# A mixture-of-experts block on one core: the 32-row activations turned by VectorE in 32x32 blocks, with weight rows dealt to partitions to match

## What is computed

```
logits = xf @ w_router + b_router            # 32 experts
top_val, top_idx = top_k(logits, 4); gates = softmax(top_val)
# for each token and each of its four experts e:
hu   = x @ w1[e] + b1[e]                      # 1024 -> 2048: gate 1024, lin 1024
gate = min(hu[:1024], 7); lin = clip(hu[1024:], -7, 7)
act  = gate * sigmoid(1.702 * gate) * (lin + 1)
out += gates[e] * (act @ w2[e] + b2[e])       # 1024 -> 1024
```

## Time and profile before

| what | value |
|---|---|
| median of 3 runs (lowest to highest) | 1412.05 us (1411.45 to 1412.62) |
| span of the profiled execution | 1411.9 us |
| TensorE busy | 1306.3 us (93%) |
| VectorE busy | 654.5 us (46%) |
| ScalarE / GpSimd busy | 292.9 / 296.0 us (21% each) |
| bytes moved by DMA | 459.19 MB |
| first `up` matmul | at 367.8 us of the span |

### The profile page before, as it was taken

One profiled execution on the slowest core, in us unless ns is written; L12 is line 12 of the kernel. 1 busy time (PEld: TensorE's weight loads), 2 busy tenths in 40 slices (PEclk: granted clock), 3 DMA queues, 4 the chain that ended last, 5 costly groups with the idle time before them and its releaser, 6 DMA issues.

```text
span 1411.9 us, 36717 instructions
## 1 busy us (share of the span) xinstructions
PE 1306.3 (93%) x13322; PEld 635.0 (45%) x13323; DVE 654.5 (46%) x2237; ACT 292.9 (21%) x582; POOL 296.0 (21%) x475
## 2 busy tenths in 40 slices
PE   7999999989579996999999999997999799999992
PEld 4756665555134442444444444442444344444441
DVE  2114334655545552555555555553555355555555
ACT  2012223424111110111111111111111111111113
POOL 5310000002122221222222222221222122222221
PEclk9999999999789998999999999999999999999997
DMA  9520003427498999999999997999999999999994
GB/s 322 145 50 1 1 0 139 164 82 283 192 415 358 415 417 421 415 419 416 418 416 416 417 414 303 380 411 417 420 417 419 418 417 416 416 418 415 418 416 171
DMA packets 59954, 459.19 MB, mean 325 GB/s; under 512 B 8693, under 2 KB 9077, under 8 KB 27157
## 3 DMA queue, kind: packets, MB, share of 16 engines
q1 hardware_dynamic: 51364, 436.12, 74.6%
q0 software_dynamic: 8176, 22.36, 6.0%
q10 hardware_dynamic: 384, 0.32, 0.1%
HBM read 440.26 MB, written 18.51 MB: 325 GB/s over the span
## 4 chain that ended last, share of the span: by engine, by line
PE 83%; DMA 10%; DVE 3%; issue 2%; ACT 1%; POOL 0%; SPq 0%; DVEq 0%; ACTq 0%; POOLq 0%
PE PS L1682 38%; PE PS L1709 19%; DMA sb_arena<-in_w 7%; PE PS L1347 4%; PE PS L1341 4%; PE PS L1719 2%; PE PS L1344 2%; PE PS L1345 2%; PE PS L1541 2%; PE PS L1663 1%; DMA xfd<-sb_arena 1%; PE PS L1725 1%; PE PS L1689 1%; PE PS L1392 1%; PE PS L1514 1%
## 5 line engine op out<-in xcount | busy, mean ns | idle before, releaser
L1682 PE MATMUL PS<-sb_arena,sb_work 128*32 128x512 f32 x5184 | 590.0, 606 | 39.3 <-DMA sb_arena<-in_w 29.6
L1682 PEld LDWEIGHTS PS<-sb_arena,sb_work 128*32 128x32 f32 x5184 | 187.3, 112 | 391.9 <-issue 329.6
L1709 PE MATMUL PS<-sb_arena,sb_work 128*32 128x256 f32 x5184 | 298.3, 382 | 4.5
L1236 DVE TENSOR_SCALAR sb_work<-PS 128x256 f32<-128x256 f32 x81 | 34.2, 422 | 397.2 <-PE PS L1689 397.2
L1709 PEld LDWEIGHTS PS<-sb_arena,sb_work 128*32 128x32 f32 x5184 | 167.0, 110 | 112.0 <-issue 20.9
L831 ACT ACTIVATE sb_work<-PS 128x256 f32<-128x256 f32 x81 | 31.0, 383 | 816.1 <-PE PS L1719 816.1
L1249 DVE TENSOR_SCALAR sb_work<-PS,sb_gates 32x256 f32<-32x256 f32 x324 | 155.0, 478 | 11.1 <-PE PS L1709 2.0
L584 POOL TENSOR_TENSOR sb_sm<-sb_sm 128x1 f32<-128x1 f32 x85 | 16.7, 197 | 552.2 <-DVE sb_gidx L1190 547.0
L1160 DVE TENSOR_SCALAR sb_slots<-sb_ca,sb_b,sb_rk 128x128 bf16<-128x128 f32 x340 | 95.3, 368 | 59.1 <-issue 59.1
L593 POOL DMA_INDIRECT accd<-sb_work,sb_sidc x81 | 110.9, 1369 | 12.5 <-issue 1.1
L829 ACT ACT_TABLE_LOAD x81 | 103.9, 1283 | 1.4
(11 more groups left out here) (264 smaller groups left out, 1169.6 us busy)
## 6 DMA issues: line engine op xcount, KB each, us to landing
sb_arena<-in_w SPq DMA_DIRECT2D x192, 2048.0 KB, 19.7
sb_arena<-in_w_in SPq DMA_DIRECT2D x6, 2048.0 KB, 21.0
sb_arena<-in_x SPq DMA_DIRECT2D x8, 512.0 KB, 7.9
sb_arena<-in_w_out SPq DMA_DIRECT2D x2, 2048.0 KB, 11.9
accd<-sb_arena SPq DMA_DIRECT2D x4, 512.0 KB, 8.9
xfd<-sb_arena SPq DMA_DIRECT2D x4, 512.0 KB, 5.8
sb_arena<-accd SPq DMA_DIRECT2D x4, 512.0 KB, 5.4
out<-sb_arena SPq DMA_DIRECT2D x4, 512.0 KB, 3.5
```

Of the source, the lines that this page charges most:

```text
L1682: last = mm(PS[group(c), b, :].rearrange("p (a n) -> p a n", a=2), xT[:, k % 2, group(k // 2)], w[:, k, :, c, :], start=k == 0, stop=False)
L1709: last = mm(PS[group(n), 4, 0:QD], actT[:, k % 2, group(k // 2)], w[:, k, n * QD:(n + 1) * QD], start=False, stop=k == KT - 1)
```

## The change

The four PE transposes of a block and the two copies of ScalarE go. In their place VectorE turns 128x256 elements with one instruction that transposes each 32x32 block by itself. Such a turn does not move anything between partition groups, so column 32-groups of the activation end up as rows of the contraction only if the columns were dealt to the partition groups in the right way; the layouts follow from that.

- x: the columns of a token's row are written to the table in another order (`quartered(stage)` <- `quarters(res)`), and `ffn_norm` is loaded from an input that the host has permuted in the same way (`ffn_row`). The row of the last token tile, one VectorE instruction of 1024 columns, becomes four of 256.
- hidden: `up` lets partition group c have columns a*512 + c*128 + n with a = 0..3 and n < 128 (before a*1024 + c*256 + n with a = 0, 1 and n < 256). The w2 rows follow: a partition now gets four neighbouring rows, 16 KB in one piece.
- waits: `turn_rows` is inside `hidden` of the block before, between the clip and the product; `turn_hidden` of block g+1 stands behind `outputs` of block g. What waited for `xT_done` (SyncE at L482, GpSimd's gathers) waits for `xT_ready`.

```
-            return I["w2"][e, 2 * c * QD:2 * (c + 1) * QD, :].rearrange("(c p j) n -> p c j n", c=2, j=2)
+            return I["w2"][e, 2 * c * QD:2 * (c + 1) * QD, :].rearrange("(p j) n -> p j n", j=4)
...
-            sp.wait_ge(xT_done, 2)
+            sp.wait_ge(xT_ready, 2)
...
-                act.activation(stage[t % 2], res[:, t, :], ACT.Copy, scale=rinv[:, t:t + 1]).then_inc(scaled, 1)
+                act.activation(quartered(stage[t % 2]), quarters(res[:, t, :]), ACT.Copy, scale=rinv[:, t:t + 1])\
+                    .then_inc(scaled, 1)
...
-                        act.wait_ge(actT_done, g + 1)
-                        act.activation(actT, PS[:, 6, 0:QD].rearrange("p (j n) -> p j n", j=2), ACT.Copy)\
-                            .then_inc(actT_ready, 1)
...
-                        xT_copy(g + 2, b)
...
+            for q in range(Q):
+                nc.vector.scalar_tensor_tensor(quartered(stage[1])[:, q], quarters(res[:, 3, :])[:, q], rinv[:, 3:4],
+                                               quartered(gain)[:, q], ALU.mult, ALU.mult).then_inc(xf_last, 1)
...
+            def turn_rows(b, r):
+                dve.wait_ge(xg_in[b], r * 16 + 16)
+                nc.vector.transpose(xT.rearrange("p (c j) s -> p c j s", j=2),
+                                    xg[b].rearrange("p (c q j) -> p c j q", c=Q, j=2)).then_inc(xT_ready, 1)
+
+            def turn_hidden(n, b):
+                dve.wait_ge(act_ready, n + 1)
+                nc.vector.transpose(actT.rearrange("p (c j) s -> p c j s", j=4),
+                                    gat[b].rearrange("p (c q j) -> p c j q", c=2, j=4)).then_inc(actT_ready, 1)
...
                 nc.vector.tensor_scalar(lin, lin, HID_LIMIT, -HID_LIMIT, ALU.min, ALU.max).then_inc(hid_step, 1)
+                turn_rows(1 - b, r)
                 dve.wait_ge(sig_ready, n + 1)
...
                         outputs(g, b)
+                        with dve.If(g + 1 < nb):
+                            turn_hidden(g + 1, 1 - b)
+                        dve.nop()
                         selector(g + 2, b)
...
-                        last = mm(PS[group(n), 4, 0:QD], actT[:, k % 2, group(k // 2)],
+                        last = mm(PS[group(n), 4, 0:QD], actT[:, k, :],
...
-                pe.wait_ge(act_ready, g + 1)
-                for j in range(2):
-                    last = nc.tensor.transpose(PS[:, 6, j * P:(j + 1) * P], pairs(gat[b], j), ident)
-                last.then_inc(actT_done, 1)
-                turn_x(g + 2, b, i + 1)
```

69 lines of the change are left out of this document (30 added, 39 removed).

## The result

The changed kernel takes 1405.11 us (median of 13 runs, 1400.21 to 1409.34). The ratio to the kernel before is 0.9936, with a 95% interval of 0.9921 to 0.9950: some 9 us faster (7 to 11), where the forecast was 16. The median lies inside the forecast's range of 1389 to 1406, at its upper end. The profiled execution has a span of 1403.6 us, 8.3 less than before. One of the 20 executions of the kernel before that stand beside the first four experiments took 2289 us, at a granted clock of 0.602, and the ratios leave it out.

A forecast was written before the change was run, and what follows sets the result against it. The prediction took the weight loads as the bound, with TensorE close beside; +1 (start) - 5 (w2) - 7 (free time filled) - 5 (tail) = -16 from 1411.9 us gave 1396 us, range 1389 to 1406.

The forecast's parts named there:

- The start: First weight loads wait for VectorE's turn of block 1: stream 5 us later, mostly absorbed at 424 to 432; net +1 us.
- The pieces: Loads of w2 in 16 KB pieces: 0.085 us saved on each of 63 loads in the full stretches, -5 us.
- The free time from 857 on: Free DMA time from 857 to 902, 9.7 us, mostly filled because TensorE releases buffers earlier: -7 us, ends -3 and -9.7.
- the lead: How much earlier TensorE lets the load of 864.19 be issued: 8 to 9 us, so at about 855.5.
- The tail: After the last weight load lands: last `down` ends 2.3 to 2.8 us behind it instead of 7.8; -5 us.
- TensorE, 0.58 for a block: Between `up` and `down`, without the four transposes: each block 0.58 us shorter, 11.20 in place of 11.78.
- VectorE, nothing: VectorE's two turns in each block, 0.42 us each (0.3 to 1.1), are covered and add no time.
- the cover: VectorE's slack in each block before TensorE waits: 3.4 us for two turns beyond 0.36 idle; each us beyond counts 81 times.
- The second rival: TensorE's lead is lost, since new waits for weights bring slow matmuls and late buffer releases: 1406 us, chance 0.10.
- A gain per byte of DMA is worth its full size: On the kernel before: weight loads are the bound, so any saving in DMA time shortens the kernel by all of it.

The follow-up runs named there:

- after_gap_fill: Changed kernel plus 14 idle filler matmuls on TensorE behind the `down` of block 79 only; 1403.42 us, ratio 0.9928 to the kernel before.
- after_two_y: Changed kernel with two alternating PSUM banks for `down`'s result, and VectorE's hidden turn and selector ahead of the evictions; 1401.07 us, ratio 0.9901 to the kernel before.
- after_pe_turns: Changed kernel with four idle transposes put back on TensorE in each block, between `up` and `down`; 1401.50 us, ratio 0.9928 to the kernel before.
- before_w2_16k: Kernel before with only the w2 pieces changed, to one of 16 KB for a partition; 1412.18 us, ratio 1.0004 to the kernel before.
- after_w2_8k: Changed kernel with only the w2 pieces undone, back to two of 8 KB for a partition; 1407.03 us, ratio 0.9964 to the kernel before.

## Why the prediction was right in direction and wrong in size

The mechanism held: the loads bound the changed kernel. Three of the four terms of the sum were near, and one, the tail, was wrong. The terms for the profiled executions, which differ by 8.3 us:

- **The start, +1.** The load came 4.5 us later (5 foretold) and the share in 424 to 432 rose from 0.45 to 0.96, 4.1 us: net +0.4. Right in the trace; the timed runs would allow the later start to be worth up to 4.5.
- **The pieces, -5.** Measured 4.4 to 5.5 where the loads alone set the time, as foretold. In the changed kernel it is 4.0 by the ratios and less by the medians and the spans; of the 13.4 us by which the stream is shorter, the other terms (4.1 and 6.4) leave 2.9 for it.
- **The free time from 857 on, -7.** It was 9.7 and is 0.37 x 9 = 3.3: -6.4. Right in size, but by half the lead: 4.3 us at the load, not 8 to 9, so the size is in part luck. TensorE's last long wait before it, for the `up` that starts at 805.70, was followed by matmuls at half clock, 3.64 us for a quarter that took 1.92 just before, and 4.36 for a `down` of 3.63:

```profile
810.81 1.92 PE L1690 MATMUL PS<-sb_arena,sb_work 128*32 128x512 f32 x16 [1.50 <-DMA sb_arena<-in_w]
816.42 3.64 PE L1690 MATMUL PS<-sb_arena,sb_work 128*32 128x512 f32 x16 [3.69 <-DMA sb_arena<-in_w]
...
820.81 4.36 PE L1717 MATMUL PS<-sb_arena,sb_work 128*32 128x256 f32 x64
```

- **The tail, -5.** This step failed, and it is most of the miss: 6 of the 7 to 8 us between the forecast and the result. It came out at +1.1: the last `down` ends 9 us behind the last weights, not 2.3 to 2.8. The step took every duration of its chain from rows at full clock: 1.7 for the last quarter of `up`, 3.66 for the last `down`. They took 3.64 and 6.23, together 4.5 us more. And it let the evictions follow `down` of block 79 at once. VectorE was still at the lists of the next blocks until 1370.3, 1.3 us behind that `down`, since `up` had ended late. The last w1 quarter came 9.3 us ahead of the last packet and not 10.7, 1.4 more. Together these are some 7 us, about the miss of the step (9.2 for 2.3 to 2.8). after_gap_fill and the comparison of all last `down`s show the clock's part of the last `down`, 2.6 us; after_two_y shows that VectorE's chain held 2.9 us of the start of the last `down`. The part of the slow quarter of `up` was not tried by itself, since the run that aimed at it was spoilt by its code. By chance the quarter ran at full clock in after_gap_fill; the 1.7 us by which that kernel's last `down` came nearer to the last packet, beside the filler's gain, are the only measure of it.
- **TensorE, 0.58 for a block.** It was 0.83 (10.95 us by `up` at 707.18 and 718.13), nearly all of the pairs' busy time of 0.91. It didn't matter: after_pe_turns gives 0.47 of it back and loses nothing.
- **VectorE, nothing.** The turns take 0.435 and 0.647 us, inside 0.3 to 1.1. Tripled, 3.2 us in all where the prediction saw room for 3.8, they do lengthen the median block by 0.8 us, so the cover was real and a little smaller than was said; but the price of crossing it was 3 us and not 65, since blocks have slack against the loads.

Together: +0.4 - 4 - 6.4 + 1.1 = -8.9, against -8.3 in the spans (the part behind the last `down`, 24.0 us for 24.5, is in these 8.3). The second rival had the clock as its cause and 1406 as its time, and the median is 1405. It was right about the cause in the tail; its other terms (+3 at the start, -3 of the free time) were not what happened, so it comes to the right sum in part by chance. What the prediction had against it, that the clock was whole at once behind the wait of the earlier trace rows, was one case: behind other waits whole groups ran at 0.50. The rule of the Trainium skill to which the prediction gave little weight ("TensorE: Matmul & The Clock Gate", Part 1) agrees with these rows in part: matmuls behind a wait for a load often ran at the lower level here (3.64 us for a quarter of `up`), but not behind every such wait, as the quarter of 1.92 us behind 3.86 us of idle time shows.

One statement on the kernel before must be corrected. "A gain per byte of DMA is worth its full size" was wrong for it: before_w2_16k gains nothing, and in the last 260 us of that kernel TensorE never waits for a load. Once the rest of the change is in, the pieces are worth up to 4 us. The pieces need the rest of the change; the rest does not need them, since it brings 5 us alone (after_w2_8k). Of TensorE's 0.83 us the last 0.47 are worth nothing (after_pe_turns); that the first 0.36 are what moved the bound is my reading of the two runs together, not a run of its own.

## What to carry to other kernels

Where two resources are both near full, ask which one is waited for last in the final stretch, not on average: a gain on the other one shows as nothing until the first has moved. Count the tail separately, and with the rates of the tail: behind a wait for data or for another engine TensorE may run at half its clock (here 6.23 us for 3.66), so a chain made of steady-state durations comes out too short. Where the last blocks wait for a chain on another engine, put what the next matmul needs ahead of evictions that only need to be done some time.

## What the runs showed of the hardware that was not expected

- Code in a branch that is hardly ever taken can cost every turn of a loop. With 468 more matmuls and one more branch in TensorE's loop the kernel took 2271 us in place of 1405, with 415 packets on the instruction queue in place of 19; with 28 more and no further branch, nothing. Where between the two the limit lies was not tried.
- The two turns move the same 128x256 float32 elements, and take 0.435 and 0.647 us. They differ in the distance between the elements that they read, every second one for x and every fourth for the hidden row; a turn with other distances was not measured, so the cause is a guess.
- Idle transposes on TensorE, 38 us of them, made the kernel no slower (0.9928 to 0.9936), and its mean clock was higher (0.957 to 0.965 for 0.945 to 0.955): work in place of waits cost nothing.
- The clock behind a wait is not the same in each execution of the same instructions: the last quarter of `up` took 3.64 us behind 1.80 us of idle time (the changed kernel) and 1.92 behind 3.86 (after_gap_fill).
